# One stream split in two, modulation rows of two layers made on VectorE, expert weights laid out in longer runs

## What is computed

```python
for l in (0, 1):
    mx, mc = silu(c) @ ada_w[l] + ada_b[l], silu(c_ctx) @ ada_w[l] + ada_b[l]     # six rows of 1024 each
    hx = modulate(rmsnorm(x), mx[0], mx[1]); hc = modulate(rmsnorm(ctx), mc[0], mc[1])
    yx, yc = mixer_ab(hx, hc) if l == 0 else mixer_mla(hx, hc)                    # layer 1: no yc
    x = x + mx[2] * rmsnorm(yx)
    x = x + mx[5] * rmsnorm(swiglu(modulate(rmsnorm(x), mx[3], mx[4]), w13[l], w2[l]))
    if l == 0: the same two steps for ctx, with mc and the same weights
# layer 2: modulation by ada_w_2, HGRN over x with its state from ctx_2, spatial gating, then
x = x + g * moe_expert_choice(h)   # 16 experts, 32 tokens each, 3 matrices of 1024 x 2048
return rmsnorm(x)
```

## Time and profile before

| what | value |
|---|---|
| median of 3 runs | 2781.61 us (2778.0 to 2782.05) |
| the profiled execution: its own time | 2776.35 us |
| its span, first to last instruction | 2774.4 us |
| PE busy | 2235.6 us (81%) |
| DVE busy | 576.9 us (21%) |
| ACT busy | 408.5 us (15%) |
| moved by DMA | 613.17 MB, mean 221 GB/s |
| chain that ended last | PE 48%, DMA 31%, DVE 5%, ACT 1%, issue 1% |

### The profile page before, as it was taken

One profiled execution on the slowest core, in us unless ns is written; L12 is line 12 of the kernel. 1 busy time (PEld: TensorE's weight loads), 2 busy tenths in 40 slices (PEclk: granted clock), 3 DMA queues, 4 the chain that ended last, 5 costly groups with the idle time before them and its releaser, 6 DMA issues.

```text
span 2774.4 us, 25106 instructions
## 1 busy us (share of the span) xinstructions
PE 2235.6 (81%) x10537; PEld 1154.7 (42%) x10537; DVE 576.9 (21%) x1238; ACT 408.5 (15%) x814; POOL 6.2 (0%) x13
## 2 busy tenths in 40 slices
PE   6999988999999899899987789775555555565555
PEld 3444443444444446688834677641111111111111
DVE  3126823000000437200031582310000000000001
ACT  2014533000000325300032122110000000000000
POOL 0000000000000000000000000000000000000000
PEclk9999999999999999999999898987788778778876
DMA  9538841121222210243611231389999999999997
GB/s 367 219 160 307 314 138 61 61 81 42 63 78 68 91 61 31 92 151 103 201 61 61 70 112 70 129 342 418 417 416 417 418 418 418 418 416 416 417 418 300
DMA packets 198800, 613.17 MB, mean 221 GB/s; under 512 B 5360, under 2 KB 98800, under 8 KB 156448
## 3 DMA queue, kind: packets, MB, share of 16 engines
q1 hardware_dynamic: 197824, 608.28, 56.9%
q0 software_dynamic: 864, 3.28, 0.4%
HBM read 610.49 MB, written 1.05 MB: 220 GB/s over the span
## 4 chain that ended last, share of the span: by engine, by line
PE 48%; DMA 31%; DVE 5%; ACT 1%; issue 1%; DVEq 0%; ACTq 0%
PE ps L330 47%; DMA ring<-in_expert_w_up 12%; DMA ring<-in_expert_w_down 12%; DMA ring<-in_expert_w_gate 7%; PE ps L669 1%; DVE AR L635 1%; DVE X L636 1%; DVE AR L1254 0%; DVE AR L1242 0%; DVE AR L1243 0%; ACT H L581 0%; DVE AR L1135 0%; DVE AR L1231 0%; DVE AR L1232 0%; ACT RS L557 0%
## 5 line engine op out<-in xcount | busy, mean ns | idle before, releaser
L330 PE MATMUL ps<-ring,AR 128*32 128x512 f32 (+1 forms) x4096 | 523.2, 659 | 373.9 <-DMA ring<-in_expert_w_up 139.5
L330 PE MATMUL ps<-H,ring 128*128 128x512 f32 (+1 forms) x2416 | 800.5, 493 | 21.1 <-ACT H L581 13.1
L330 PEld LDWEIGHTS ps<-H,ring 128*128 128x128 f32 x2416 | 460.9, 192 | 353.2 <-issue 305.2
L330 PEld LDWEIGHTS ps<-ring,AR 128*32 128x32 f32 x4096 | 144.6, 134 | 735.8 <-issue 257.9
L330 PE MATMUL ps<-AR,ring 128*128 128x256 f32 (+1 forms) x1024 | 299.6, 456 | 3.0 <-DVE AR L793 1.5
L330 PEld LDWEIGHTS ps<-AR,ring 128*128 128x128 f32 x1024 | 196.1, 192 | 106.2 <-issue 84.4
L330 PE MATMUL ps<-AR 128*64 128x128 f32 (+5 forms) x1168 | 213.8, 340 | 29.6 <-DVE AR L1243 9.5
L330 PEld LDWEIGHTS ps<-AR 128*128 128x128 f32 (+2 forms) x1168 | 151.0, 186 | 108.9 <-issue 81.2
L1653 DVE TENSOR_TENSOR AR<-AR,ps 128x512 f32<-128x512 f32 x16 | 11.0, 688 | 590.9 <-PE ps L330 590.9
L793 DVE TENSOR_TENSOR AR<-AR,ps 128x512 f32<-128x512 f32 (+1 forms) x44 | 24.4, 555 | 424.7 <-PE ps L330 424.7
L1639 ACT ACTIVATE AR<-ps 128x512 f32<-128x512 f32 x16 | 9.6, 597 | 548.8 <-PE ps L330 548.8
(11 more groups left out here) (220 smaller groups left out, 1100.3 us busy)
## 6 DMA issues: line engine op xcount, KB each, us to landing
ring<-in_expert_w_gate SPq DMA_DIRECT2D x64, 2048.0 KB, 24.0
ring<-in_expert_w_up SPq DMA_DIRECT2D x64, 2048.0 KB, 23.4
ring<-in_expert_w_down SPq DMA_DIRECT2D x64, 2048.0 KB, 23.9
ring<-in_ada_w SPq DMA_DIRECT2D x36, 2048.0 KB, 8.6
ring<-in_ffn_w SPq DMA_DIRECT2D x44, 1024.0 KB, 7.1
ring<-in_ffn_w SPq DMA_DIRECT2D x16, 1408.0 KB, 7.1
ring<-in_w_in SPq DMA_DIRECT2D x11, 2048.0 KB, 7.9
ring<-in_ab_w_in SPq DMA_DIRECT2D x4, 2048.0 KB, 15.9
```

What stands on the lines that cost most here:

```text
L330: m = nc.tensor.matmul(out_, lhsT=lhsT, rhs=rhs, start=start, stop=stop)
```

## The change

**Two streams.** `Pre` and `Post` take one half each (256 columns, x or ctx), with signals of their own. PE's 8 calls of ones in `Pre` become a fold on DVE (`dve_fold`, 7 additions) and one call. The input projection is ordered by `AB_ORDER`, ctx ahead of x; its last six x items run beside the ctx attention. The attention is split into 24 ctx units and 24 x units, b units first; subln runs beside them, and the ctx output projection beside the x units. In ffn 0 ctx runs two blocks ahead of x, every product on 256 columns. The load of ctx2 and its norm move beside the w2 chunks of ffn 1.

**Modulation rows.** The 24 `ada` jobs of layers 1 and 2 become 24 `row` jobs of the same 2 MB (512 rows, 1024 columns, 4 KB runs), one behind each w13 load and one behind the first w2 load, for layer 1 in ffn 0 and for layer 2 in ffn 1. DVE multiplies and accumulates them per partition, PE sums over partitions by ones. The jobs 6 to 11 of layer 0 move into the ctx attention.

**Expert weights.** `runs` puts consecutive rows on one partition: 2 rows for `gu`, 4 for `dn`, 16 KB of consecutive memory for either. Strides in the expert code follow.

```diff
+        def runs(w, r0, r1):
+            k, n = (r1 - r0) // P, w.shape[-1]
+            return (lambda s: ring[:, s, 0:k * n].rearrange("p (k n) -> p k n", k=k),
+                    w[r0:r1, :].rearrange("(p k) n -> p k n", p=P))
...
+        def row_job(l, n):
+            w = A["ada_w"][1] if l == 1 else A["ada_w_2"][0]
+            job(("row", l, n), rows(w, n % 2 * 512, (n % 2 + 1) * 512, n // 2 * 1024, (n // 2 + 1) * 1024))
...
-                job(("gu", e, i), rows(w, (i % 4) * 256, (i % 4 + 1) * 256, 0, EF))
+                job(("gu", e, i), runs(w, (i % 4) * 256, (i % 4 + 1) * 256))
...
-                job(("dn", e, i), rows(A["expert_w_down_2"][0, e], i * 512, (i + 1) * 512, 0, D))
+                job(("dn", e, i), runs(A["expert_w_down_2"][0, e], i * 512, (i + 1) * 512))
...
+        def dve_row_job(c, l, n):
+            if n % 2 == 0 and n:
+                dve_row_copy(c, l, n // 2 - 1)
+            if n % 2 == 1 and n > 1:
+                dve_row_turned(c, l, n // 2 - 1)
...
+            conds = 2 if n < 4 else 1
+            for kk in range(4):
+                for cond in range(conds):
+                    by = SC[:, 4 * (n % 2) + kk, l // 2, cond:cond + 1]
+                    if n % 2 + kk == 0:
+                        ins = V.tensor_scalar(acc[:, cond, :], w[:, kk, :], by, None, ALU.mult)
+                    else:
+                        ins = V.scalar_tensor_tensor(out=acc[:, cond, :], in0=w[:, kk, :], scalar=by, in1=acc[:, cond, :],
+                                                     op0=ALU.mult, op1=ALU.add)
...
+        def pe_row_job(pe, l, n):
+            if n < 12:
+                pe.wait_ge(row_done.sem, 12 * (l - 1) + n + 1)
+                used()
+            if n % 2 == 1:
...
+                for half in range(2):
+                    for cond in range(conds):
+                        j = 32 * (2 * half + cond)
+                        mm(ps[j:j + 32, b, :], ones[:, 0:32], acc[:, cond, half * 512:(half + 1) * 512], True, True,
...
+            elif n:
+                b = take(pe, ("rowsT", l, n // 2 - 1))
+                freed(pe, ("rows", l, n // 2 - 1))
+                for i in range(4):
+                    m = nc.tensor.transpose(ps[:, b, i * P:(i + 1) * P], RS[:, i * P:(i + 1) * P], ident)
...
+        def dve_norms(c, post, pre):
+            for k in range(KD):
+                post.dve_add(c, k)
+                if k >= 2:
+                    pre.dve_fold(c, k - 1)
+            pre.dve_fold(c, KD - 1)
+            pre.dve_scale(c)
...
+        def pe_ffn0(pe):
+            for s, i in FFN0:
+                row = i - LAG if s == 1 and i >= LAG else None
...
+                if (s, i) == (1, 0):
+                    post0a[0].pe(pe)
+                if (s, i) == (1, 1):
+                    pre0f[0].pe(pe)
+                if (s, i) == (0, NW + KD - LAG):
+                    post0f[1].pe(pe)
+                if (s, i) == (0, NW + KD - LAG + 1):
+                    pre1a[1].pe(pe)
...
+        def dve_ffn1(c):
+            for i in range(NW):
+                dve_rows_beside(c, 2, i)
+                dve_w13(c, 1, i, 0, i)
...
+        AB_ORDER = [(1, 0), (1, 1), (1, 2), (0, 0), (1, 3), (0, 1), 4, 5, (1, 4), (0, 2)]
+        AB_BESIDE = {0: 10, 2: 11, 4: 12, 6: 13, 8: 14, 10: 15}
+        ADA_BESIDE = {13: 6, 14: 7, 16: 8, 17: 9, 18: 10, 19: 11}
...
+        def pe_beside_x(pe, i):
+            if i % 2 and i < 16:
...
+                pe_out_chunk(pe, "yc", "ab_out_ctx", n, lambda k: H[:, k, TX:T2])
+            pe_subln_beside(pe, 0, i)
...
+        def pe_mla_kv(pe, s, pre):
...
+            for j in range(2):
+                pe_dense(pe, ("lk", s, j), w, j * P, H[:, :, HALF[s]], TX, pre=pre if j == 0 else None)
+                if s == 1 and j == 0:
+                    post0f[0].pe(pe)
...
+            act_norms(c, post0a[1], pre0f[1])
+            for k in range(KD):
+                post0a[0].act_chunk(c, k)
+            act_norms(c, post0a[0], pre0f[0])
+            act_ffn0(c)
```

More of the change, by code:

```diff
@@ L543, in act_squares, with row_acc @@
-        def act_squares(c, base, chunks, src, sq, wait):
-            for k in range(chunks):
-                wait(c.eng, k)
-                c.mark(S.activation(sq(k), src(k), ACT.Square), squares_ready, base + k + 1)
+        def row_acc(l, n):
+            both = n < 4
+            at = 13056 if l == 2 else 13312 if both else 13824
+            return ar(at, 2 if both else 1, 1024)
+        def dve_row_job(c, l, n):
[3 more added lines that the diff above has]
+                dve_row_turned(c, l, n // 2 - 1)
+            j = job_at[("row", l, n)]
+            c.eng.wait_ge(slot_loaded[j % SLOTS], loaded_at[j])
+            w = ring[:, j % SLOTS, :].rearrange("p (k n) -> p k n", k=4)
+            acc = row_acc(l, n)
+            conds = 2 if n < 4 else 1
[7 more added lines that the diff above has]
+                                                     op0=ALU.mult, op1=ALU.add)
+                    if kk == 3 and cond == conds - 1:
+                        c.mark(ins, row_done, 12 * (l - 1) + n + 1)
+                    else:
+                        c.step(ins)
@@ new lines, in pe_w13 @@
+        def pe_w13(pe, l, i, s, pre=None, row=None):
+            w = weights(pe, ("w13", l, i)).rearrange("p (k n) -> p k n", k=KD)
+            for g, name in enumerate("gu"):
+                if g and row is not None:
+                    pe_row_job(pe, l + 1, row)
+                b = take(pe, (name, l, i, s))
+                for j in range(2):
+                    for k in range(KD):
+                        if pre is not None and g + j == 0:
+                            pre.ready(pe, k)
+                        mm(ps[:, b, j * TX:(j + 1) * TX], w[:, k, g * 256 + j * P:g * 256 + (j + 1) * P],
+                           H[:, k, HALF[s]], k == 0, k == KD - 1, b if j and k == KD - 1 else None)
+            if s == 0:
+                used()
@@ new lines, in pe_w2 @@
+        def pe_w2(pe, l, n, s, name, row=None):
+            w = weights(pe, ("w2", l, n))[:, 0:KF * P].rearrange("p (k n) -> p k n", k=KF)
+            if n == 0:
+                freed(pe, ("u", l, KF // 2 - 1, s))
+            b = take(pe, (name, n))
+            for k in range(KF):
+                mm(ps[:, b, 0:TX], w[:, k, :], hid(l)[:, k, HALF[s]], k == 0, k == KF - 1, b if k == KF - 1 else None)
+                if k == KF // 2 and row is not None and row <= 12:
+                    pe_row_job(pe, l + 1, row)
+            if s == 0:
+                used()
@@ new lines, in pe_out_chunk, with pe_out @@
+        def pe_out_chunk(pe, name, label, n, Hf):
+            w = weights(pe, (label, n // 4)).rearrange("p (k n) -> p k n", k=KD)
+            b = take(pe, (name, n))
+            for k in range(KD):
+                mm(ps[:, b, 0:TX], w[:, k, n % 4 * P:(n % 4 + 1) * P], Hf(k), k == 0, k == KD - 1, b if k == KD - 1 else None)
+            if n % 4 == 3:
+                used()
+        def pe_out(pe, name, label, Hf, wait):
+            wait(pe)
+            for n in range(KD):
+                pe_out_chunk(pe, name, label, n, Hf)
@@ new lines, in build @@
+        pre1a = [Pre(("pre1a", s), 1, 0, s, (12288, 13056)[s]) for s in range(2)]
+        lat_rs, krope, qrope = rstd_ready[0].plan(2), roped.plan(1), roped.plan(8)
+        attn1 = Attention(mla_units, lambda pe, i: None, lambda c, i: None, lambda c, i: None)
+        post1a = Post("y1", 1, 0, 0, lambda k: y1[:, k, :], 10240)
+        pre1f = Pre("pre1f", 1, 1, 0, 10240)
+        post1f = Post("ffn1", 1, 1, 0, lambda k: yg[:, k, :], 10240)
+        pre2a = [Pre(("pre2a", s), 2, 0, s, (10240, 12288)[s]) for s in range(2)]
```

901 lines of the change are left out of this document (533 added, 368 removed).

## The result

The changed kernel takes 2800.71 us (median of 4 runs, 2798.45 to 2804.07) against 2781.83 of the kernel before (4 runs, 2778.0 to 2782.35): a ratio of 1.0072, 95% interval 1.0054 to 1.0089. The forecast was 2703, 98 us less, and the range ended at 2750. The profiled execution took 2798.45 us, with a span of 2795.7.

What follows compares the result with a forecast made beforehand. PE was taken to bound the kernel up to 1811 us and the loads to bound the experts after. Terms from -44 (input projection) to +16.6 (attention) summed to -79, from 2781.6 to 2703 us, range 2672 to 2750.

Steps and rivals of the forecast that it cites:

- the attention: Layer 0 attention with subln: PE the limit on the whole, 191.5 us where 174.9 were taken before, +16.6.
- the bound of 205: Layer 0 attention: upper bound of 205 us, a bubble of 15%, beside a lower bound of 178 for perfect packing.
- Rival 2: Attention: the clock falls to 1.2 GHz in the last a units of each stream, +40, 2743 us; chance 0.10.
- Rival 6: Attention: something other than PE paces it, so nothing shortens it; whole near no change, 2782 us; chance 0.02.
- Rivals 1: Expert loads: the long runs give nothing, all else stands, 2724 us; chance 0.20.
- 5: Expert loads: the new address pattern lowers the rate; half way to 295 GB/s gives 2914 us; chance 0.05.
- rival 3: Feed-forwards: row work on DVE not covered, about 1 us in each of 24 jobs, 2727 us; chance 0.06.
- Rival 4: Attention and expert loads: both do better, packing at 180 us or 4.83 us per load, 2682 us; chance 0.08.
- ffn 0 with y0: First y0 chunk to end of ffn 0: -42.1 up to ffn 0 and +12.3 in it, together -29.8.
- post0f and pre1a: Norms between ffn 0 and the next attention: 28.7 us becomes 19, -6.2.
- the loads: Expert stage: 16 KB runs as one packet save on average 0.117 us per load over 184 loads, -21.5.
- The prediction's estimate of 68 us more: Ffn 0: the skill's 512-column rule taken as a 15% loss would add some 68 us; not used in the sum.

Runs made afterwards that it cites:

- kernel 9: Kernel 5 with the two attentions of layer 0 run as one list of 48 units: 2718.14 us, ratio 0.9776 to the kernel before.
- Experiments 1: The changed kernel with VectorE's side work done one unit later, after the next unit's probabilities: 2756.69 us.
- kernel 5: The changed kernel with VectorE's side work one unit later and all scores three units ahead: 2723.07 us, timed repeat 2723.86 us.
- 6: The changed kernel with only the scores of the two-map units given three units ahead: 2775.76 us.
- kernel 10: A run whose edit and measured time are not described in the text given.
- experiments 7: Kernel 5 with the experts' weights loaded in rows of 4 or 8 KB as in the kernel before: 2747.32 us.
- 8: The kernel before with only the experts' loads taken from the change (16 KB runs and strided columns): 2753.93 us.

## Why the prediction was wrong

**The step that failed** is the attention: "So PE is the limit on the whole, but not everywhere", from 178 us of work on PE against 147 on DVE, with 4 us for the b heads and 4.5 for each pipeline's start. Both totals were right: PE 181.86 us in kernel 9, and DVE 131.46 in 404 instructions, which with 0.04 between two is near 148. What was not looked at is the order of each queue. The text stated as a premise that the larger total ends last. It never followed one unit through `dve` and `pe` to ask which instruction of one engine stands behind which of the other, though the diff has both facts: side work of unit i on both engines in the same slot, and the lookahead cut to two. Where the prediction had PE paced by its own work, the runs showed one chain through both engines: the attention took 281.95 us, not 191.5, with 64.3 us of idle PE and 217.65 us of PE work. Experiments 1, 5 and 6 show that these two orders cost 75 of the 90.5 missing us (72 by kernel 10's trace), in waits and in a lower granted clock.

**What is left** of this term: with both orders mended it is 206.5 to 210 us, 15 to 18 over the forecast and above the bound of 205. Of the 15 us of kernel 5, some 7 are PE's busy time (184.73 against 178) and 8 its idle time (21.8 against the 13 added). The trace of kernel 5 shows 4.8 and 3.8 us at the two starts as counted, but the first side item behind the first of them takes 5.99 us, mostly at 1.2 GHz, and the last units of each stream have nothing beside them. ScalarE's side work stands in the same slot as PE's too, and no run moved it; PE waits 6.4 us for ScalarE in kernel 5, so it can explain part of this at most. Kernel 9 brings the attention to 202.2. The bound itself was misread: 205 was called half as much again as the bubble in attn0, but 9.7 idle us to 150.8 busy are 6.4%, and 15% is over twice that. Even this bound was far too low.

**The rivals.** Rival 2 (the clock falls in the attention) named one of the two parts and missed its place. PE's busy time is 39.7 us over the 178 counted, which is the 40 us of this rival, but by luck: the fall was put into the last a units, and it came with the first units already (0.75 from 152 to 200 us, 0.90 from 400 to 433). The other 51 us are idle time, which the rival left out. Rival 6, that something other than PE paces the attention, had 0.02 and comes nearest to what happened (its 2782 us supposed no change in the attention; it got 107 us longer); "PE busy 150.8 of 160.5 us" was evidence from the kernel before, where the ada jobs needed nothing of VectorE but two copies in eight units and the scores were three ahead. The change replaced just that. Rivals 1 and 5 are excluded by the rows, 4.90 us per load, and by experiments 7 and 8; rival 3 by PE busy 243.32 of 244.3 us in feed-forward 1 with all its row jobs, where none of its waits is for a row operation. Rival 4 did not come: its packing was the contrary.

**Right, by their own steps**: ffn 0 with y0 (505.65; predicted 535.0 - 29.8 = 505.2), post0f and pre1a, post1a and pre1f, the row jobs on PE, their cover on DVE, and the loads (-21.2; 21.5 predicted, and 21.5 by experiment 7). The input projection came 4 us longer than summed, ffn 1 by 2, and the saving at post1f and pre2a was 2 smaller. Also right: the packets, and the loads over 184 of them (5.05 less 0.117 is 4.93, as measured). Two slips of the sums are too small to matter: 178, 4 and 9 add to 191, not 191.5, and 15.5 less 9.55 is 5.95, not 6.3.

**The two rules.** Columns of 256 in place of 512 cost no 15%: 505.65 us against 505.2 for the sum at 0.217 us per instruction, and PE's 2306 instructions of this stretch took 498.14 us, 0.216 each. The Trainium skill (TensorE: Matmul & The Clock Gate, Why this matters for your kernels) asks for all dimensions of 512 and more, and 20 GFLOP in all, for 85% of peak. The prediction's estimate of 68 us more took this as a rule for the columns of one instruction; taken so, the trace disagrees.

The loads of the experts, in kernel 5:

```profile
1824.95 1.92 PE L358 MATMUL ps<-ring,AR 128*32 128x512 f32 x16 [0.93 <-DMA ring<-in_expert_w_gate]
...
1844.56 2.78 PE L358 MATMUL ps<-ring,AR 128*32 128x512 f32 x16 [2.88 <-DMA ring<-in_expert_w_up]
```

These two starts are four loads apart, 4.90 us per 2 MB or 428 GB/s. The Trainium skill (DMA: Bandwidth & Descriptors, Where 436 GB/s comes from) has 435 as the ceiling of the fabric, and the trace agrees with it as a ceiling not reached. The same section of the Trainium skill also says that for loads from HBM a limit of about 358 GB/s per core binds, which the prediction did not mention; here the measurement decides, and this one core loaded faster than that.

## What to carry to other kernels

Adding up the work of each engine gives a floor, not a forecast: where two engines hand work to each other every few microseconds, follow one unit through both instruction lists, and look for a wait that stands ahead of something already possible. Side work that comes back from the other engine should be collected one unit later than it is sent; what feeds the next unit should be issued ahead of it. A change that takes filler work off the limiting engine, or lays new work beside a chain, deserves this above all, and a slip in the order is cheap to mend: two edits of a few lines turned 19 us lost into 57 gained (2781.25 against 2723.86).

## What was not expected of the hardware

The clock made the order costlier than the waits alone. The same item of 16 instructions on 256 columns took 5.41 us in the changed kernel and 3.72 in kernel 5, and over the whole attention PE's busy time fell from 217.65 to 184.73 us for nearly the same instructions, so about 33 of the 75 us regained were clock, not waits. In the changed kernel PE waited 32 times ahead of the transposes, 1.9 us on average and 5.3 at most, and the granted clock was 0.83 over the stretch; in kernel 5 it waited 8 times there, of which only the two waits at the starts of the streams, 4.8 and 3.8 us, were over 1.2 us, and the clock was 0.95. That the waits caused the lower clock, and nothing else that differs, is the reading that fits these kernels; it was not tried by itself. Two gains that each shorten the same chain gave more together than apart (75.5 against 42.1 + 21.6 us): of the near 12 us between, 5 are in PE's busy time and 6 in its idle time. That either wait alone hides behind the other is the likely reading of the latter, not shown.
